# Last quad of experts and the hand-over to block 2: first slabs of block 2 behind a wait, up products ahead of the sums, eight products of constants in place of sixteen

## The reference

```python
def hier_moe(h, ..., w_gate, w_up, w_down, w_sh_gate, w_sh_up, w_sh_down):
    ...
    a = jnp.einsum('nd,edf->nef', t, w_gate)          # 32 experts, d 1024, f 256
    b = jnp.einsum('nd,edf->nef', t, w_up)
    hid = jax.nn.silu(a) * b * combine[:, :, None]
    routed = jnp.einsum('nef,efd->nd', hid, w_down)
    shared = (jax.nn.silu(t @ w_sh_gate) * (t @ w_sh_up)) @ w_sh_down
    return (routed + shared).reshape(bsz, slen, d)

# first_block ends with
    h = h + rms_norm(ffn, post_ffn_norm[l])
# second_block begins with
    h = rmsnorm(x, norm_mix_g[l])
    proj = h @ w_in[l]                                # 1024 x 7168
```

## Time and profile before

| | |
|---|---|
| median of 3 runs | 884.06 us (883.14 to 885.74) |
| profiled execution, its own time | 883.84 us |
| its span in the profile | 882.2 us |
| TensorE busy | 799.1 us, 91% |
| VectorE, ScalarE, GpSimd busy | 55%, 43%, 5% |
| chain that ended last | TensorE 68%, DMA 16%, VectorE 6%, ScalarE 5%, issue 3% |
| HBM read | 203.87 MB |

### The profile page before, as it was taken

One profiled execution on the slowest core, in us unless ns is written; L12 is line 12 of the kernel. 1 busy time (PEld: TensorE's weight loads), 2 busy tenths in 40 slices (PEclk: granted clock), 3 DMA queues, 4 the chain that ended last, 5 costly groups with the idle time before them and its releaser, 6 DMA issues.

```text
span 882.2 us, 13432 instructions
## 1 busy us (share of the span) xinstructions
PE 799.1 (91%) x5491; PEld 635.4 (72%) x5491; DVE 482.6 (55%) x799; ACT 383.0 (43%) x650; POOL 47.7 (5%) x114
## 2 busy tenths in 40 slices
PE   6997999997868676879999999999999999999995
PEld 5986789663434332459989876678878999999974
DVE  6777667210110030074936787677676666666675
ACT  5574767210000100065447755665344544444454
POOL 5000120100100011000000000000000000000000
PEclk9999999998898888899999999999999999999998
DMA  9960193999999999996418543346556555555101
GB/s 278 376 230 31 49 349 108 393 378 421 421 421 421 421 421 421 408 340 205 143 50 333 190 156 109 131 138 235 181 186 191 184 183 182 184 181 187 45 1 48
DMA packets 77998, 205.81 MB, mean 233 GB/s; under 512 B 5720, under 2 KB 48896, under 8 KB 65648
## 3 DMA queue, kind: packets, MB, share of 16 engines
q1 hardware_dynamic: 69454, 150.44, 48.0%
q0 software_dynamic: 8480, 54.49, 15.4%
q10 hardware_dynamic: 2, 0.00, 0.0%
HBM read 203.87 MB, written 1.05 MB: 232 GB/s over the span
## 4 chain that ended last, share of the span: by engine, by line
PE 68%; DMA 16%; DVE 6%; ACT 5%; issue 3%; SPq 0%; POOL 0%; ACTq 0%; DVEq 0%
DMA big<-in_w_up 13%; PE ps L2045 11%; PE ps L2046 10%; PE ps L2047 10%; PE ps L1867 8%; PE ps L1869 7%; PE ps L1868 7%; PE ps L2193 5%; DMA big<-in_w_down 3%; PE ps L2172 1%; PE ps L2207 1%; ACT WH L659 1%; ACT WH L650 1%; PE ps L2410 1%; PE ps L2424 1%
## 5 line engine op out<-in xcount | busy, mean ns | idle before, releaser
L1156 DVE TENSOR_TENSOR WL<-big,WH 128x1024 fp32r<-128x1024 f32 x154 | 186.6, 1222 | 95.9 <-ACT WH L659 95.3
L659 ACT ACTIVATE WH<-big 128x1024 fp32r<-128x1024 f32 x154 | 160.4, 1053 | 62.7 <-PE ps L2047 62.2
L1867 PE MATMUL ps<-XH,WH 128*128 128x256 f32 (+1 forms) x640 | 185.2, 289 | 1.1 <-DVE XL L1221 0.6
L1869 PE MATMUL ps<-XH,WL 128*128 128x256 f32 (+1 forms) x640 | 182.7, 285 | 0.0
L1868 PE MATMUL ps<-XL,WH 128*128 128x256 f32 (+1 forms) x640 | 182.6, 285 | 0.0
L1867 PEld LDWEIGHTS ps<-XH,WH 128*128 128x128 f32 x640 | 123.2, 193 | 4.0 <-issue 2.1
L1868 PEld LDWEIGHTS ps<-XL,WH 128*128 128x128 f32 x640 | 123.3, 193 | 0.8
L1869 PEld LDWEIGHTS ps<-XH,WL 128*128 128x128 f32 x640 | 123.2, 192 | 0.0
L2193 PE MATMUL ps<-big 128*32 128x256 f32 x1024 | 76.5, 465 | 42.2 <-DMA big<-in_w_gate 26.2
L2045 PE MATMUL ps<-WH,XH 128*128 128x512 f32 x240 | 99.0, 413 | 1.5 <-ACT big L983 1.2
L2193 PEld LDWEIGHTS ps<-big 128*32 128x32 f32 x1024 | 42.1, 133 | 77.8 <-issue 66.7
(11 more groups left out here) (399 smaller groups left out, 1085.9 us busy)
## 6 DMA issues: line engine op xcount, KB each, us to landing
big<-in_w_in SPq DMA_DIRECT2D x35, 1024.0 KB, 9.6
big<-in_w_gate SPq DMA_DIRECT2D x16, 1024.0 KB, 14.4
big<-in_w_up SPq DMA_DIRECT2D x16, 1024.0 KB, 14.8
big<-in_w_gate POOLq DMA_DIRECT2D x16, 1024.0 KB, 18.8
big<-in_w_up POOLq DMA_DIRECT2D x16, 1024.0 KB, 19.5
big<-in_w_down SPq DMA_DIRECT2D x16, 1024.0 KB, 15.3
big<-in_w_down POOLq DMA_DIRECT2D x16, 1024.0 KB, 19.6
big<-in_w_mlp_up SPq DMA_DIRECT2D x16, 1024.0 KB, 5.4
```

Of the source, the lines that this page charges most:

```text
L659: s.activation(dst, src, ACT.Copy).then_inc(ev("unit_high"), 1)
L1156: v.tensor_tensor(dst, src, h.bitcast(F32), ALU.subtract).then_inc(ev("unit_split"), 1)
L1867: mm(o, h, rh, start=first, stop=False, skip_group_check=skip)
L1869: return mm(o, l, rh, start=False, stop=last, skip_group_check=skip)
```

## The change

SP waits, ahead of block 2's first slab, until slabs 9 and 11 of the last quad (the down weights that GpSimd issues) have landed. In the last quad TensorE does the up products straight after the gate products, then the sums of quad 6 and the turning, as in the other quads; eight products of constants stand behind the wait for the turned hidden values, ahead of the down products, and the sixteen behind the gate products are gone.

```diff
--- before.py
+++ after.py
@@ -498,6 +498,8 @@
                     sp.dma_start(s.rearrange("p (c n) -> p c n", c=2), pcn(w[j * 256:(j + 1) * 256, c0:c0 + D]))\
                         .then_inc(slab2(m)[0], 16)
 
+            for s in (9, 11):
+                sp.wait_ge(*slab_e(QUADS - 1, s))
             for m in range(RING2):
                 sp.wait_ge(ev("expert_slab_used"), RING * (QUADS - 1) + m + 1)
                 second_slab(m)
@@ -2286,9 +2288,6 @@
                 x = lambda c: xg[:, o % 2, c, half * SLOTS:(half + 1) * SLOTS]
                 wait_slots(q, 0)
                 gate_or_up(0, 0, x).then_inc(ev("expert_slab_used"), QUAD)
-                if q == QUADS - 1:
-                    combine_rows(q - 1)
-                    keep_busy(16, 0)
                 if o + 1 < OCTETS:
                     pe.wait_ge(ev("sel_ready"), o + 3)
                     pe.wait_ge(ev("xg_by_vector"), 8 + 2 * q)
@@ -2302,13 +2301,14 @@
                     pe.wait_ge(ev("rows_by_vector"), q)
                     pe.wait_ge(ev("sel_w_ready"), o + 1)
                     turn_weights()
-                if q < QUADS - 1:
-                    combine_rows(q - 1)
+                combine_rows(q - 1)
                 pe.wait_ge(ev("hidden_ready"), q + 1)
                 turn_hidden().then_inc(ev("hidden_turned"), 1)
                 pe.wait_ge(ev("hidT_ready"), q + 1)
                 if half == 0:
                     pe.wait_ge(ev("sel_T_ready"), o + 1)
+                if q == QUADS - 1:
+                    keep_busy(8, 0)
                 wait_slots(q, 2 * QUAD)
                 down(2 * QUAD).then_inc(ev("expert_slab_used"), QUAD)
             pe.wait_ge(ev("rows_by_scalar"), QUADS)
```

## The result

| | kernel before | changed kernel |
|---|---|---|
| median of 20 runs | 883.15 us | 887.26 us |
| profiled execution, own time | 883.84 us | 888.4 us |
| span in the profile | 882.2 us | 886.7 us |

The ratio is 1.0046, with a 95% interval from 1.0034 to 1.0058: the changed kernel is 3.0 to 5.1 us slower, 4.1 us by the medians. The forecast was +4.3 us and, from the 884.06 us of the first three runs, 888.4 us in all. One of the changed kernel's 20 runs took 940.01 us and is not in the ratio; the others lie between 884.86 and 888.68 us.

The account below looks back on a forecast made before the run. TensorE was taken as the bound from about 393 us, passing on any hand-over delay. Down products at 378.0 instead of 373.69 gave +4.3 us: 883.84 to 888.2, plus 0.2 for the median, 888.4 us; range 885.8 to 890.0.

Parts of the forecast that it names:

- main theory: Last quad: up products at the lower clock and eight constants delay the down products; 887.9 to 888.8 us, chance 0.64.
- rival A: Last quad's up products: clock holds or comes back early, so +2.1 to +3.4 us (886.1 to 887.5); chance 0.15.
- Steps 1 to 5: TensorE's last quad: up products wait, run slowly, then sums, turning, constants; down products at 378.0 instead of 373.69 us.
- steps 2 and 5: Last quad: up products at the lower clock take 5.89 us; eight constants ahead of the down products take 2.1 us.
- Step 6: SP's wait: slab 11 lands 0.4 us sooner (0 to 1 us), at 373.2; not in the sum.
- Step 7: Block 2's first slab: issued about 373.3, lands 378.4, split at 382.7; costs nothing, about 0.5 us late without cover.
- Rival B: Last quad: up slabs ready by 361, so TensorE hardly waits; 883.0 to 884.1 us, chance 0.07.
- Rival C: Block 2's first slab takes more than 9.4 us and ScalarE waits; 890.0 to 895.8 us, chance 0.06.
- Rival D: SP's wait changes nothing for the down slabs, landing at 373.6; still 888.4 us, included in the forecast's 0.64.
- step 5: Eight constants between copy and down products cost 2.1 us on the path; the sixteen removed lay in a wait.

## Why the prediction was right, point by point

Times are after the start of the last gate products; the forecast's are the text's less 354.44.

| step | forecast | changed kernel |
|---|---|---|
| 1. up products start | 11.3 | 11.36 |
| 2. they take (start to next start) | 5.89 | 5.79 |
| 3. up's end (next start) to turning | 3.44 | 3.54 |
| 4. turning to the next products | 0.91 | 0.91 |
| 5. eight constants | 2.1 | 2.03 |
| down products start | 23.6 | 23.63 |
| 7. ScalarE's first split | 28.3 | 28.34 |
| first unit product | 43.3 | 43.30 |

The forecast of the time, 888.4 us, was 1.1 us too high all the same, because the kernel before has a median of 883.15 us over 20 runs and not the 884.06 of its first three. So the measured 887.26 us lie below the band of the main theory (887.9 to 888.8) and in that of rival A, although the trace shows the main theory's mechanism: the bands were narrower than the base was known.

**Steps 1 to 5** held one by one, and the sum with them: no term is off by more than 0.1 us, and the differences nearly cancel. The kernel that puts the constants into the gap fixes steps 2 and 5 at once and gets 3.95 of the 4.40 us back; the kernel with SP's wait alone and the one with TensorE's order alone place the loss wholly on TensorE.

**Step 6** was right in direction and near in size. Issues of the down slabs 9 and 11 with their landings, in the changed kernel; the second is issued 0.53 us after the first:

```profile
big<-in_w_down POOLq DMA_DIRECT2D x1, 1024.0 KB, 21.3
...
big<-in_w_down POOLq DMA_DIRECT2D x1, 1024.0 KB, 23.2
```

Slab 11 lands 2.4 us after slab 9. Over the kernels with SP's full wait this distance is 2.4 to 2.8 us (six kernels), over those in which w_in goes out early 2.9 to 4.0 us (five, the kernel before with 2.9 and the two with the first slab free with 2.9 and 3.0 among them). From the gate products' start slab 11 lands after 18.6 us in the changed kernel and 19.1 in the kernel before. Over the six kernels with the full wait it is 18.5 to 19.0 us, over the other five 19.0 to 19.3, by the medians 0.4 us sooner, as I took it; with only the first slab let through (two kernels) it is 19.1, no gain. As said there, it bought nothing in the changed kernel, because nobody waited for it. That it "would be worth its 0.4 us" if TensorE's part were free holds only if the hidden values come earlier as well, and in the kernel before they are ready together with the slab. A kernel with both, early hidden values and SP's full wait, was not run.

**Step 7**, the first slab:

```profile
373.57 18.57 SPq L492 DMA_DIRECT2D big<-in_w_in  x8
big<-in_w_in SPq DMA_DIRECT2D x1, 1024.0 KB, 5.3
```

It was issued at 373.57, landed 5.3 us later and was split at 383.18 with 0.41 us of idle time named issue: covered, as the sum had it. Its price without cover was set too low: 0.5 us forecast, 0.8 us in the kernel with SP's wait alone, where the slab took 5.5 us.

**Rival A** (a warmer start of the up products) did not occur in the changed kernel, but its size was right: at the upper clock the up products take 3.66 us. The Trainium skill ("TensorE: Matmul & The Clock Gate", What's actually happening) says that the number of slow products varies from run to run. The traces agree: quad 6's up products, up to which all kernels here are the same, took 5.35 to 6.33 us. The last quad's, behind idle times of 4.67 to 5.65 us, took 5.18 to 6.05 us; here the longest idle time goes with the shortest products and the shortest with the longest, so a longer wait didn't mean a dearer start. **Rival B** is out: the up products of the changed kernel name the DMA as their releaser after 4.95 us, and the constants in the gap brought them no nearer. **Rival C** is out by the 5.3 us. **Rival D**'s premise, no gain for the down slabs, is not borne out, and was of no weight.

**What the text had wrong beside the sum** is a remark in step 5: that the sixteen constants "lay in a wait", which the expectations for the kernel without them took to mean that they were of no use. They lay in a wait, and cost nothing there; but without them the wait moves to the place ahead of the down products and lowers the clock for these, at 1.4 us. The prediction did not need this, because in the changed order the down products follow other work at once.

**What stays open.** The first unit product of the kernel with SP's wait alone comes 20.50 us after its down products instead of 19.65; 0.8 of these 0.85 us stand in ScalarE's wait, the rest was not followed. Why the landing of the last up slab, counted from the gate products' start, is 10.0 us in the kernel before without constants and 11.0 to 11.4 us in the others stays open too; in that profile GpSimd's first up slab landed 2.7 us ahead of SP's second, in the others 0.2 to 0.5 us. Each kernel has one profile, so a difference of some 0.5 us between two stretches can be the start of one group at the lower clock. And what the clock does behind the down products, at the norm, was seen but not explained.

## What to carry to other kernels

On an engine that works in order, moving a group forward is worth only what its data allow: ask first when its last input lands, and what the engine did until then. Products of constants were free only in a wait that existed anyway; one place further they cost their full time, while the wait they left behind cost the clock of what followed it. Filling one wait may open another further down, so look at the idle time ahead of every group up to the point where the chain is a transfer.

## What the runs showed of the hardware

- Idle times of 1.02 and 3.80 us, or of 1.03 and 2.10 us, each pair with 0.5 us of work between, were followed by a lower clock for the next products (5.04 and 5.34 us instead of 3.64); 1.03 and 0.63 us in the kernel before, and 0.92 us behind constants, were not. The expectation for that kernel had no price for such a wait.
- The same products behind the same kind of wait took 5.18 to 6.05 us over five kernels at the lower clock, and 3.66 us at the upper one.
- Stopping another queue's small transfers (1 KB each) brought a 1 MB transfer of GpSimd's queue in only some 0.4 us sooner (medians over six and five kernels), at a DMA share of 1.0; letting one 1 MB transfer of them through took the gain away (two kernels). From the shares in the earlier trace rows up to 1 us had been estimated.
